# ScalarE copies both pairs of the turned keys of each sample unit out of PSUM; VectorE copies none

## The reference

```python
def mix_layer(h, pos, mstate, gstate, window_fn, sb_fn, ...):
    (aq, ak, av, ai, af, ao, bq, bk, bv, bg, blr,
     cq, ck, cv, dq, dk, dv) = split_columns(h @ w_in)
    mstate, ha = run_chunks(mlstm_chunk, mstate, (qa, ka, va, ig, lf))
    gstate, hb = run_chunks(gla_chunk, gstate, (qb, kb, vb, la))
    hc = window_fn(qc, kc, vc)      # samples: cached rotary keys, then the new ones
    hd = sb_fn(qd, kd, vd, b_sb)    # samples: z = q k^T / 8 + bias over 16 pages, then the new keys
    return concat(ha, hb, hc, hd) @ w_out, ...
```

## Time and profile before

| | |
|---|---|
| runs, us | 2412.24, 2414.48, 2419.23 (median 2414.48) |
| profiled execution, us | 2420.88 |
| its span, us | 2419.2 |
| mean granted PE clock | 0.973 |
| key copies on ScalarE (L2753) | 104 |
| key copies on VectorE (L2814) | 104 |

### The profile page before, as it was taken

The page is one execution under the profiler, slowest core; times in us unless marked ns, Lnnn a source line. Parts: engine busy times, 40 slices in busy tenths (PEclk is TensorE's granted clock), DMA queues, the critical chain, the costliest instruction groups (busy, mean ns, idle before and its releaser), DMA issues. The chain is left out here.

```text
span 2419.2 us, 44912 instructions
## 1 busy us (share of the span) xinstructions
PE 2279.2 (94%) x17646; PEld 2065.4 (85%) x17646; DVE 1199.8 (50%) x2114; ACT 924.3 (38%) x1637; POOL 147.1 (6%) x197
## 2 busy tenths in 40 slices
PE   7999999999888799999999999999998888999997
PEld 7999999777556599999999999988775557999997
DVE  6433265336665555342453333753466654743425
ACT  5223252324435554222452233432243455632333
POOL 0000010002222000000000000100112200000000
PEclk8999999999989899999999999999898999999999
DMA  5323334226866543232333233431467746332333
GB/s 134 82 69 92 100 98 151 71 88 189 251 188 181 173 126 82 69 97 78 105 76 101 69 87 93 124 120 53 132 207 231 239 132 196 88 88 69 87 104 93
DMA packets 384957, 290.97 MB, mean 120 GB/s; under 512 B 51808, under 2 KB 368392, under 8 KB 384272
## 3 DMA queue, kind: packets, MB, share of 16 engines
q1 hardware_dynamic: 368128, 234.08, 34.2%
q0 software_dynamic: 16128, 54.54, 7.2%
q10 hardware_dynamic: 528, 0.02, 0.0%
HBM read 274.99 MB, written 13.58 MB: 119 GB/s over the span
## 5 line engine op out<-in xcount | busy, mean ns | idle before, releaser
L222 PE MATMUL ps<-h_hi,w_hi 128*128 128x288 f32 x2400 | 716.7, 299 | 16.4 <-PEq L177 10.4
L223 PE MATMUL ps<-h_lo,w_hi 128*128 128x288 f32 x2400 | 708.2, 295 | 0.0
L224 PE MATMUL ps<-h_hi,w_lo 128*128 128x288 f32 x2400 | 708.1, 295 | 0.0
L222 PEld LDWEIGHTS ps<-h_hi,w_hi 128*128 128x128 f32 x2400 | 450.4, 188 | 23.7 <-issue 16.9
L246 DVE TENSOR_TENSOR w_lo<-w_raw,w_hi 128x2048 fp32r<-128x2048 f32 x143 | 327.8, 2292 | 262.0 <-ACT w_hi L240 261.6
L223 PEld LDWEIGHTS ps<-h_lo,w_hi 128*128 128x128 f32 x2400 | 450.6, 188 | 1.0
L224 PEld LDWEIGHTS ps<-h_hi,w_lo 128*128 128x128 f32 x2400 | 450.3, 188 | 0.0
L240 ACT ACTIVATE w_hi<-w_raw 128x2048 fp32r<-128x2048 f32 x143 | 272.9, 1908 | 125.9 <-PE ps L224 77.5
L222 PE MATMUL ps<-f_a_hi,w_hi 128*128 128x288 f32 x1024 | 302.7, 296 | 0.0
L224 PE MATMUL ps<-f_a_hi,w_lo 128*128 128x288 f32 x1024 | 301.6, 295 | 0.0
L223 PE MATMUL ps<-f_a_lo,w_hi 128*128 128x288 f32 x1024 | 301.5, 294 | 0.0
(11 more groups left out here) (365 smaller groups left out, 3226.1 us busy)
## 6 DMA issues: line engine op xcount, KB each, us to landing
w_raw<-in_w_ffn_in SPq DMA_DIRECT2D x132, 512.0 KB, 5.2
w_raw<-in_w_ffn_out SPq DMA_DIRECT2D x80, 512.0 KB, 4.9
sa_vn<-in_cache_sb_v SPq DMA_DIRECT2D x256, 128.0 KB
w_raw<-in_w_in SPq DMA_DIRECT2D x52, 512.0 KB, 4.5
sa_vn<-in_cache_win_v SPq DMA_DIRECT2D x96, 128.0 KB
w_raw<-in_w_out SPq DMA_DIRECT2D x24, 512.0 KB, 7.6
sa_kn_early<-in_cache_win_k POOLq DMA_DIRECT2D x72, 128.0 KB
sa_vn<-in_cache_win_v SPq DMA_DIRECT2D x16, 512.0 KB
```

Of the source, the lines that this page charges most:

```text
L222: pe.matmul(out, stat_hi, mov_hi, start=start, stop=False, skip_group_check=True)
L223: pe.matmul(out, stat_hi, mov_lo, start=False, stop=False, skip_group_check=True)
L224: return pe.matmul(out, stat_lo, mov_hi, start=False, stop=stop, skip_group_check=True)
```

## The change

ScalarE, after its copy of pair a, waits for `turned_b` and copies pair b too, from bank 5, and it is ScalarE that frees the bank. VectorE's tick no longer calls `copy_keys_b`. PE's order, the transposes, GpSimd, SyncE and all other instructions stay.

```diff
     def copy_keys_a(act, n):
         e = ev_a["k", n]
         act.wait_ge(S["turned_a"], e + 1)
         if n >= 2:
             act.wait_ge(S["scores_done"], G["scored"]["unit", n - 2])
         act.activation(kt[:, n % 2, 0], ps[:, TURN_A[e % len(TURN_A)], :], ACT.Copy).then_inc(S["free_a"], 1)
+        act.wait_ge(S["turned_b"], ev_b["k", n] + 1)
+        act.activation(kt[:, n % 2, 1], ps[:, TURN_B[ev_b["k", n] % len(TURN_B)], :], ACT.Copy).then_inc(S["free_b"], 1)
@@ vector_tick
             spread_queries(dve, True)
-        if t < U:
-            copy_keys_b(dve, t)
         for c in chunks:
             if c["tick"] == t:
                 take(dve, c)
```

## The result

The changed kernel took 2397.37 us (median of 7 runs, 2396.29 to 2405.04), the kernel before 2414.48 (7 runs, 2400.89 to 2420.92); the ratio of the means is 0.9939, with a 95% interval of 0.9911 to 0.9967. That is 17 us by the medians and 15 us, or 0.6%, by the means; 4.4 us were forecast, and the range ended at 2401. The profiled execution took 2397.74 us, its span is 2396.1.

A forecast was written before the change was run, and what follows sets the result against it. PE was taken as the bound, busy for 94% of the span. Gains of 0.8 + 0.5 + 0.9 = 2.2 us a layer, 4.4 in both, came off the 2414.5 us median: 2410 us, range 2401 to 2421.

The forecast's parts named there:

- where VectorE holds up PE: PE's waits behind VectorE's key copy: L2003 and L2035 start 0.60 us sooner each, units 29 and 32 give 0.7 together.
- some 4 us ... either way: PE's granted clock in a layer's ticks: some 4 us hang on where it falls, named under the rival VectorE ahead.
- the loss of unit 6: ScalarE's added copy pushes L1770, for which PE already waits 0.46 us: PE loses 0.5 us.
- at 600.55: PE waits 0.89 us to turn an odd weight chunk into bank 5; ScalarE would end the key copy 0.54 us sooner.
- at 569.77: PE's gap of 0.85 us, hanging on a take that starts 0.5 earlier without VectorE's copy; unit 6's loss ends there.
- 739.07: Prompt attention: PE waits 0.79 us on the chain of L2304 behind the key copy; 0.5 us gain taken.
- 752.04: Prompt attention: PE waits 1.00 us for L2324 behind the same chain as at 739.07; 0.9 us gain taken.
- units 9 and 13: Two units where ScalarE's added copy delays PE, by up to 0.48 us each; 0.7 us loss taken together.
- I keep half: PE's DMA wait at 732 us: of 1.5 us gained before it, 0.8 is kept, with 0 and 1.5 as ends.
- ScalarE becomes the late engine: Rival: all ten pushes of a layer by ScalarE's added copies reach PE, 10 us slower, 2424.5 us; chance 14%.
- VectorE runs ahead: Rival: without the mid-tick wait VectorE's gaps on PE close entirely, 16 us faster, 2398.5 us; chance 16%.
- Nothing moves: Rival: DMA wait and ScalarE's pushes take the gains back, within 1 us of 2414.5 us; chance 20%.

The follow-up runs named there:

- e6: Kernel before, with ScalarE copying pair b only in units 30, 32 and 34 of each layer; 2401.9 us, ratio to before 0.9962.
- e10: The changed kernel run again without further edit, beside the kernel before; 2397.6 us, ratio 0.9939.
- e3: Kernel before, with ScalarE copying pair b only in units 36 to 51 of each layer; 2414.4 us, ratio to before 1.0001.
- e4: Changed kernel, but VectorE still waits in each tick for PE's transposes of pair b and copies nothing; 2401.3 us, ratio to before 0.9948.

## Why the prediction was wrong

**The step that failed** is the gain "where VectorE holds up PE": L2003 "starts 672.97 - 672.37 = 0.60 sooner", L2035 "likewise", "of 2 x 0.60 I take 0.7" for two more. The shortening came as said at the first two, 0.60 and 0.59; of the 0.7 for the two more 0.25 came, in unit 32, and 0.03 in unit 29. What failed is that a wait of PE was priced at its own length, so that the clock behind it stood in the sum at nothing. Behind these waits PE ran at 1.2 GHz in 17 of 30 places, behind the shorter ones in 3 of 48: 2.9 us of waits in both layers were worth 9.4 (e6). The clock did stand in the prediction, as "some 4 us ... either way" under a rival, that is as chance around the sum instead of a term of it. The trace of before had it in view: 0.93 in the earlier trace rows is 0.07 x 269 = 19 us lost to half clock in one layer's ticks, and the matmuls right behind the waits of the earlier trace rows run in it.

**The terms that were right.** ScalarE's copy at 591 ns for 586; the loss of unit 6 at 0.48 for 0.5; at 600.55 a gain of 0.63 for 0.54; at 569.77 the gap fell from 0.83 (second trace of before) to 0.21; 739.07 gave 0.49 for 0.5 and 752.04 0.91 for 0.9. The column "rest" of e10, -5.4 with a standard error of 1.3, agrees with the 4.4 forecast, which held waits alone. That the sum fits so well is in part luck: the gain of units 29 and 32 was too high by 0.4 a layer, but so was ScalarE's cost, as of the 0.7 lost in units 9 and 13 only 0.10 shows on PE, in unit 9.

**Not settled: the DMA wait at unit 40.** "I keep half" can't be judged: the wait was 1.93, 1.76, 2.50 and 3.11 us in the four layers of before's two profiles and 2.81, 3.35, 2.41 and 2.09 in the changed kernel's. Half clock behind the longer of these waits was not in the sum either. Nor is it settled that prompt attention pays: e3 gives 3.4 us in "rest" and nothing in time.

**The rivals.** "ScalarE becomes the late engine" fell: PE loses 0.48 in unit 6, 0.26 in unit 35 and little elsewhere. "VectorE runs ahead" had the time (2398.5) through gaps that "close entirely"; they kept 1.02 and 0.92, and e4 shows that the freedom from the wait is worth little. "Nothing moves" fell by the time. Beside it the prediction cites Perfetto Trace Analysis, Optimizing Scalar/DVE Operations, in the Trainium skill, by which offloading to ScalarE may make sense if VectorE is saturated. Here VectorE was at 62% in that stretch (167 of 269 us), and the offload paid all the same, as three of its copies stood in front of work that PE waited for.

## What to carry to other kernels

Before summing up waits, look at PE's granted clock in windows of a few microseconds around each: a wait that is often followed by half clock costs what the stretch behind it costs too, and a microsecond taken from such waits was worth about three here (9.4 / 2.9; 1.6 to 4.7 by the interval of e6). Count it place by place, since the length of a wait alone did not tell. Find the few instructions in front of such waits first: three of 52 copies carried most of this change (9.4 of 14.9 us), and reordering them on their own engine gave half of it. And take a second profile of the kernel before: one execution held 5.7 us of waits that the next didn't have.

## What was not expected of the hardware

At the same three steps the clock of TensorE (PE) fell behind waits of 1.5 to 1.6 us in 17 of 30 places and behind 0.9 to 1.3 in 3 of 48, while at another step it fell behind none of 28 waits of 1.38 or 1.39 us. TensorE: Matmul & The Clock Gate, HAM oscillation, in the Trainium skill describes such a fall to half clock in a kernel whose matmuls wait for DMAs. These traces agree (20 of 21 waits of over 2 us for values at unit 40), and here it came behind waits for VectorE as well. In one profile of fourteen, takes right behind VectorE's copy began up to 1.02 us after everything that they wait for in the trace; its cause is open.
